# Sample attention of a two-layer encoder kernel: two groups of four heads on 64 partitions, or one group with two heads above each other on 128

## The reference

```
dots  = einsum('bqhd,bsd->bqhs', qi, ik_all)           # indexer: 8 heads x 64
score = einsum('bqhs,bqh->bqs', relu(dots), wi)
top_val, top_idx = top_k(where(admissible, score, -inf), k_top)
logits = einsum('bqngd,bqknd->bqngk', qg, k_sel) * HEAD_DIM ** -0.5   # 8 heads, 2 KV heads
p = softmax(where(valid, logits, -inf))
o = einsum('bqngk,bqknd->bqngd', p, v_sel)
```

## Time and profile before

| what | value |
|---|---|
| runs | 1450.54, 1449.7, 1452.48 us |
| profiled execution | 1449.31 us, its span 1447.5 us |
| busy TensorE / VectorE / ScalarE / GpSimd | 1253.6 / 569.4 / 368.4 / 152.4 us |
| chain that ended last | PE 69%, DVE 11%, DMA 7%, ACT 6%, issue 3% |
| mean granted TensorE clock | 0.914 of full speed |
| attention, layer 0 / layer 1 | about 314 to 416 us / about 1021 to 1121 us of the span |

### The profile page before, as it was taken

How to read it: one execution, slowest core, us unless ns; L and a number is a source line. 1 busy time by engine, 2 the same in 40 slices (tenths; PEclk the granted TensorE clock), 3 DMA queues, 4 the chain that set the end, 5 groups by cost and what they waited for, 6 DMA issues and landing times.

```text
span 1447.5 us, 16324 instructions
## 1 busy us (share of the span) xinstructions
PE 1253.6 (87%) x6291; PEld 733.4 (51%) x6291; DVE 569.4 (39%) x1478; ACT 368.4 (25%) x861; POOL 152.4 (11%) x218
## 2 busy tenths in 40 slices
PE   4898699987889998999837989899686999999990
PEld 0452254543545586777523533454345457777760
DVE  1227689123236531111107257980323455111115
ACT  2214120035741111111114133001468111111111
POOL 0312050010000150000020113200100011000002
PEclk7899899997999999999967989899858999999995
DMA  9428997260960479999953120224121016799985
GB/s 362 133 69 324 352 341 228 82 228 5 313 230 30 160 211 386 356 369 365 325 184 115 59 71 30 65 67 137 35 56 25 0 68 221 252 365 361 369 289 210
DMA packets 136887, 283.95 MB, mean 196 GB/s; under 512 B 11581, under 2 KB 91877, under 8 KB 130409
## 3 DMA queue, kind: packets, MB, share of 16 engines
q1 hardware_dynamic: 116128, 208.66, 42.7%
q0 software_dynamic: 8352, 42.50, 8.5%
q10 hardware_dynamic: 12329, 31.74, 6.2%
HBM read 236.86 MB, written 52.40 MB: 200 GB/s over the span
## 4 chain that ended last, share of the span: by engine, by line
PE 69%; DVE 11%; DMA 7%; ACT 6%; issue 3%; SPq 2%; ACTq 1%; POOLq 0%; POOL 0%; DVEq 0%
PE ps L508 44%; PE ps L813 9%; PE ps L518 5%; PE ps L671 3%; DMA W<-in_w_gate 3%; PE ps L732 3%; ACT arena L1194 2%; SPq L419 2%; DMA X<-in_x_sample 2%; DVE arena L1498 2%; PE ps L859 2%; DVE small L1497 1%; DVE arena L1537 1%; DVE arena L1588 1%; PE ps L632 1%
## 5 line engine op out<-in xcount | busy, mean ns | idle before, releaser
L508 PE MATMUL ps<-W,arena 128*128 128x256 f32 (+1 forms) x1280 | 348.1, 428 | 10.3 <-DMA W<-in_w_up 5.2
L508 PEld LDWEIGHTS ps<-W,arena 128*128 128x128 f32 x1280 | 242.2, 193 | 85.4 <-issue 49.9
L508 PE MATMUL ps<-W,hT 128*128 128x512 f32 (+3 forms) x480 | 195.0, 563 | 9.7 <-DVE gt L1369 6.6
L518 PE MATMUL ps<-C,arena 128*128 128x128 f32 (+3 forms) x835 | 118.4, 282 | 55.6 <-DVE arena L1417 18.1
L813 PE MATMUL ps<-W,hT 128*128 128x512 f32 (+1 forms) x320 | 144.7, 606 | 5.7 <-ACT hT L1251 5.7
L518 PEld LDWEIGHTS ps<-C,arena 128*128 128x128 f32 (+3 forms) x835 | 95.6, 148 | 96.6 <-issue 36.1
L508 PEld LDWEIGHTS ps<-W,hT 128*128 128x128 f32 (+1 forms) x480 | 87.4, 186 | 110.3 <-issue 83.4
L508 PE MATMUL ps<-hT,W 128*128 128x128 f32 (+1 forms) x512 | 129.4, 414 | 7.1 <-ACT arena L1118 7.1
L508 PEld LDWEIGHTS ps<-hT,W 128*128 128x128 f32 x512 | 79.1, 193 | 58.4 <-issue 50.5
L1805 DVE TENSOR_TENSOR arena<-arena,ps 128x256 f32<-128x256 f32 x32 | 13.5, 421 | 221.7 <-ACT arena L1292 221.7
L813 PEld LDWEIGHTS ps<-W,hT 128*128 128x128 f32 (+1 forms) x320 | 57.1, 183 | 79.9 <-issue 73.6
(11 more groups left out here) (250 smaller groups left out, 1174.1 us busy)
## 6 DMA issues: line engine op xcount, KB each, us to landing
W<-in_w_ada SPq DMA_DIRECT2D x48, 1024.0 KB, 7.4
W<-in_w_gate SPq DMA_DIRECT2D x32, 1024.0 KB, 10.6
W<-in_w_up SPq DMA_DIRECT2D x32, 1024.0 KB, 13.1
W<-in_w_down SPq DMA_DIRECT2D x32, 1024.0 KB, 7.8
y_d<-arena ACTq DMA_DIRECT2D x33, 512.0 KB, 7.3
W<-in_w_in SPq DMA_DIRECT2D x16, 1024.0 KB, 8.5
arena<-x_d SPq DMA_DIRECT2D x31, 512.0 KB, 11.5
arena<-arena SPq DMA_DIRECT2D x128, 79.2 KB, 2.1
```

Source lines behind the costliest of these rows:

```text
L508: ins = T.matmul(out, l, r, start=n == 0, stop=n == len(pairs) - 1, skip_group_check=True)
L518: count(T.transpose(o, i, ident[0:m, 0:m]), done if n == len(outs_ins) - 1 else None)
```

## The change

The sample's eight heads become one group, so `GROUPS` has nine members: 0 and 1 are tile 0, 2 is the sample, 3 and 4 are tile 3, 5 and 6 tile 2, 7 and 8 tile 1. A job of the sample's group is now two heads: the first head's 64 queries lie on partitions 0 to 63 of a bank, the second's on 64 to 127, each written by its own matmuls (same row half of the array, other column half). Masks, exponentials, scaling and turns of this group work on 128 partitions, the copies to `pT` are 512 wide, and each product with the values has 128 columns (two heads). The mask is copied once to partitions 64 to 127. The ada parts run at steps 1 to 8 (they were at 2 to 9). The square root is still at step 7 and the block of loads still at step 3.

```diff
-        GROUPS = [(t, g) for t in ATTN for g in range(2)]
+        GROUPS = [(t, g) for t in ATTN for g in range(2 if t < 4 else 1)]
...
-            return job % 3 if job < 8 else job % 2 if job < 16 else (job + 2) % 3
+            return job % 2 if GROUPS[job // 4][0] == 4 else job % 3
...
-                            pe.wait_ge(L["ttr"], job - 1 if 2 <= n <= 4 else job - 2)
-                        q = qT[hp, i, tokens(t)]
+                            pe.wait_ge(L["ttr"], job - 1 if 2 <= n <= 3 else job - 2)
                         if t == 4:
-                            T.matmul(ps[2 + job % 2][0:DEC, 0:DEC], q, kT[1][hp, 1024:1088], start=True, stop=True)
-                        T.matmul(ps[logit_bank(job)][0:rows_of(t), 0:b - a], q, kT[1][hp, a:b], start=True, stop=True).then_inc(L["lgt"], 1)
+                            for side in range(2):
+                                rows, q = slice(64 * side, 64 * side + DEC), qT[hp, 2 * (j // 2) + side, tokens(t)]
+                                T.matmul(ps[2 + job % 2][rows, 0:DEC], q, kT[1][hp, 1024:1088], start=True, stop=True, skip_group_check=True)
+                                ins = T.matmul(ps[logit_bank(job)][rows, 0:b - a], q, kT[1][hp, a:b], start=True, stop=True, skip_group_check=True)
...
-                    if l == 0 and 2 <= n < 6:
-                        pe.wait_ge(L["ttr"], 16)
-                        ada(ps[3], U_ADA4, range(2 * (n - 2), 2 * (n - 2) + 2), 3)
-                    if l == 0 and n >= 6:
+                    if l == 0 and 1 <= n < 5:
+                        pe.wait_ge(L["ttr"], 12)
+                        ada(ps[3], U_ADA4, range(2 * (n - 1), 2 * (n - 1) + 2), 3)
+                    if l == 0 and n >= 5:
...
-                            heads = pT[0:kn, c, 0:4 * m].rearrange("p (a g t) -> p a g t", a=2, g=2)
                             for a in range(2):
-                                ins = T.matmul(ps[6 + n % 2][64 * a:64 * a + 64, q * m:(q + 1) * m], v, heads[:, a, q, :],
+                                if t < 4:
+                                    heads = pT[0:kn, c, :].rearrange("p (a q t) -> p a q t", a=2, q=2)[:, a, q, :]
+                                else:
+                                    heads = pT[0:kn, c, :].rearrange("p (j q a t) -> p q a j t", j=2, q=2, a=2)[:, q, a]
+                                ins = T.matmul(ps[6 + n % 2][64 * a:64 * a + 64, q * P:(q + 1) * P], v, heads,
...
-                        S.copy(pT[0:kn, c, 0:4 * m], ps[4 + job % 2][0:kn, 0:4 * m]).then_inc(L["pta"], 1)
+                        S.copy(pT[0:kn, c, :], ps[4 + job % 2][0:kn, :]).then_inc(L["pta"], 1)
...
-                    if l == 0 and n == 7:
+                    if l == 0 and n == 6:
                         keep_mod(3)
...
                             chain(V.tensor_scalar(sc, sc, MARK, -BIG, ALU.not_equal, ALU.mult))
+                            if t == 4:
+                                chain(V.tensor_copy(msk[64:64 + DEC, MSK_AT[t]:MSK_AT[t] + n], sc))
```

More of the change, by code:

```diff
@@ L311, in u_tail @@
             return ps[7][:, at:at + P].rearrange("p (a c) -> p a c", a=2)
-        GROUPS = [(t, g) for t in ATTN for g in range(2)]
-        PT0 = [sum(len(chunks_of(t)) for t, _ in GROUPS[:n]) for n in range(11)]
+        GROUPS = [(t, g) for t in ATTN for g in range(2 if t < 4 else 1)]
+        PT0 = [sum(len(chunks_of(t)) for t, _ in GROUPS[:n]) for n in range(len(GROUPS) + 1)]
         def logit_bank(job):
-            return job % 3 if job < 8 else job % 2 if job < 16 else (job + 2) % 3
+            return job % 2 if GROUPS[job // 4][0] == 4 else job % 3
         def rope(eng, E, rows, r, t0, t1, heads, scratch, s_chain, n_chain, done, count):
@@ L727, in logits @@
                         if job >= 3:
-                            pe.wait_ge(L["ttr"], job - 1 if 2 <= n <= 4 else job - 2)
-                        q = qT[hp, i, tokens(t)]
+                            pe.wait_ge(L["ttr"], job - 1 if 2 <= n <= 3 else job - 2)
                         if t == 4:
-                            T.matmul(ps[2 + job % 2][0:DEC, 0:DEC], q, kT[1][hp, 1024:1088], start=True, stop=True)
-                        T.matmul(ps[logit_bank(job)][0:rows_of(t), 0:b - a], q, kT[1][hp, a:b], start=True, stop=True).then_inc(L["lgt"], 1)
+                            for side in range(2):
[3 more added lines that the diff above has]
+                        else:
+                            ins = T.matmul(ps[logit_bank(job)][:, 0:b - a], qT[hp, i, tokens(t)], kT[1][hp, a:b], start=True, stop=True)
+                        ins.then_inc(L["lgt"], 1)
                 tj = [0]
@@ L760, in _ @@
                         o = bank_for_turn()
-                        turn([(o[0:kn, i * m:(i + 1) * m], PR[0:m, 4 * (n % 2) + i, c * P:c * P + kn]) for i in range(4)], L["pt"])
+                        turn([(o[0:kn, i * P:(i + 1) * P], PR[:, 4 * (n % 2) + i, c * P:c * P + kn]) for i in range(4)], L["pt"])
                     if n + 2 < len(GROUPS):
                         logits(n + 2)
-                    if l == 0 and 2 <= n < 6:
-                        pe.wait_ge(L["ttr"], 16)
-                        ada(ps[3], U_ADA4, range(2 * (n - 2), 2 * (n - 2) + 2), 3)
-                    if l == 0 and n >= 6:
+                    if l == 0 and 1 <= n < 5:
+                        pe.wait_ge(L["ttr"], 12)
+                        ada(ps[3], U_ADA4, range(2 * (n - 1), 2 * (n - 1) + 2), 3)
+                    if l == 0 and n >= 5:
                         pe.wait_ge(s_adae, 5)
-                        ada(ps[3], U_ADA5, range(2 * (n - 6), 2 * (n - 6) + 2), 4)
+                        ada(ps[3], U_ADA5, range(2 * (n - 5), 2 * (n - 5) + 2), 4)
                     if n >= 2:
@@ L1203, in normalised @@
                         h = S_INV + 4 * (n % 2) + i
-                        r = PR[0:m, 4 * (n % 2) + i, 0:NKEYS[t]]
-                        ins = S.mul(r, r, small[0:m, h:h + 1])
+                        r = PR[:, 4 * (n % 2) + i, 0:NKEYS[t]]
+                        ins = S.mul(r, r, small[:, h:h + 1])
                     ins.then_inc(L["pn"], 1)
@@ L1210, in outputs @@
                     t, g = GROUPS[n]
-                    m = rows_of(t)
                     act.wait_ge(L["pv"], n + 1)
-                    S.copy(hT[:, g:g + 3:2, t * P:t * P + m],
-                           ps[6 + n % 2][:, 0:2 * m].rearrange("p (j t) -> p j t", j=2)).then_inc(L["on"], 1)
+                    o = ps[6 + n % 2][:, 0:2 * P]
+                    if t < 4:
+                        ins = S.copy(hT[:, g:g + 3:2, t * P:t * P + P], o.rearrange("p (j t) -> p j t", j=2))
+                    else:
+                        ins = S.copy(hT[:, 0:4, t * P:t * P + DEC], o.rearrange("p (j t) -> p j t", j=4))
+                    ins.then_inc(L["on"], 1)
                 exps(0)
@@ L1252, in _ @@
                                  scale=vT[:, 44 + c:45 + c]).then_inc(L["mixy"], 1)
-                outputs(9)
+                outputs(len(GROUPS) - 1)
                 if l == 0:
@@ L1577, in masked @@
                     t, g = GROUPS[n]
-                    m = rows_of(t)
-                    mk = C[0:m, K_M0:K_M0 + P] if t == 0 else msk[0:m, MSK_AT[t]:MSK_AT[t] + NKEYS[t]]
+                    m = P
+                    mk = C[:, K_M0:K_M0 + P] if t == 0 else msk[:, MSK_AT[t]:MSK_AT[t] + NKEYS[t]]
                     if n >= 2:
@@ L1590, in masked @@
                         if t == 4:
-                            ins = V.tensor_tensor_reduce(r[:, 512:576], ps[2 + job % 2][0:m, 0:DEC], mk[:, 512:576], 0.125, MARK,
+                            ins = V.tensor_tensor_reduce(r[:, 512:576], ps[2 + job % 2][:, 0:DEC], mk[:, 512:576], 0.125, MARK,
                                                          ALU.add, ALU.max, small[0:m, mx + 4:mx + 5])
@@ L1605, in inverses @@
                 def inverses(n):
[L1606 to L1608 removed]
+                    m = P
+                    s, q = S_SUM + 4 * (n % 4), S_INV + 4 * (n % 2)
                     dve.wait_ge(L["pexp"], n + 1)
@@ L1624, in _ @@
                         masked(n + 2)
-                    if l == 0 and n == 5:
+                    if l == 0 and n == 4:
                         add_bias(3, 3)
```

18 lines of the change are left out of this document (6 added, 12 removed).

## The result

The changed kernel takes 1432.22 us (median of four runs, 1425.78 to 1435.82) where the kernel before takes 1450.13 us beside it (four runs): a ratio of 0.9863 with a 95% interval of 0.9829 to 0.9897 (it is not the quotient of the two medians, which is 0.9876). The profiled execution took 1431.55 us, its span is 1429.7 us (17.8 us less than before).

A forecast was written before the change was run, and what follows sets the result against it. It took the attention's chain of waits round three engines, none full, as the bound, its speed hanging on TensorE's clock. 1449.31 - 7.9 - 8.9 + 3.6 + 2.2 + 0.5 = 1438.8, with 1.2 for the median 1440.0 us; range 1433 to 1448.

The forecast's parts named there:

- e2 later by: Start of group 2's (the sample's) exponentials, delayed by the second column half of each logits job: +0.6 us, bounds 0 and +2.0.
- e2 to e3: From the start of group 2's exponentials to group 3's (tile 3's first half): a period of 7.6 us.
- e3 to e4: From group 3's exponentials to group 4's (tile 3's second half), with group 2's five chunks: 13.6 us layer 0, 12.8 layer 1.
- e4 to e5: From group 4's exponentials to group 5's, with the sample's values: 9.0 us in layer 0, 9.4 in layer 1.
- step with the loads: Step 3, behind tile 2's first exponentials: the block of loads' stall comes back there, costing 2.5 us (layer 0), 2.1 (layer 1).
- the step behind it: The period after the step with the loads: same work as before, 7.5 us in layer 0 and 6.6 in layer 1.
- end of stage, longer by: Last exponentials to the Silu, with more work ahead of the square root: 3.6 us longer in layer 0, 2.2 in layer 1.
- the mask's copy: VectorE's copy of the mask, 0.45 us: costs 0.5 us in layer 1, 0 (or 0.5) in layer 0.
- Rival (a): The clock hardly drops in the attention, some 8 to 9 us less: 1431 to 1435 us; chance 0.12.
- rival (b): The sample's logits column halves run one after another, +1.4 us a layer: 1443 to 1444 us; chance 0.10.
- Rivals (c) to (e): Low clock past the sample's values, 1447, chance 0.10; no measurable change, 1449 to 1451, 0.06; slower, 1460, 0.04.
- (e): Slower: after the end of stage the output projection starts and stays at 1.2 GHz; 20 us more a layer gives 1460; chance 0.04.

The follow-up runs named there:

- its fillings: Kernel before plus three unread 128x512 matmuls in the wait of step 1's logits and three in step 2, both layers: 1444.6 us, ratio 0.9971.
- the combined kernel: Changed kernel with square root at step 6, seven transfers spread over steps 3 to 6, three unread matmuls in step 1's wait: 1417.43 us, ratio 0.9772.
- the first filling: Three unread 128x512 matmuls in step 1's wait, both layers; changed kernel with moved square root and spread loads: 1417.43 us with them, 1420.72 without.

## Why the prediction missed its range

**Direction and mechanism were right, one term was mis-sized.** The periods, in us, of the predicted steps and the profiled execution:

| term | layer 0: predicted, measured | layer 1: predicted, measured |
|---|---|---|
| e2 later by | 0.6, 0.1 | 0.6, 0.1 |
| e2 to e3 | 7.6, 7.78 | 7.6, 7.79 |
| e3 to e4 | 13.6, **9.73** | 12.8, **11.57** |
| e4 to e5 | 9.0, 9.42 | 9.4, 8.22 |
| step with the loads (old period plus 2.5, 2.1) | 11.2, 10.87 | 9.9, 10.97 |
| the step behind it (as before: 7.5, 6.6) | 7.5, 7.49 | 6.6, 7.35 |
| end of stage, longer by | 3.6, 3.82 | 2.2, 2.04 |

**The step that failed is "from e3 to e4".** For layer 0 I had TensorE at 1.2 GHz through the ada part, the values and the five chunks (8.7 us behind e3), and took "the middle, 4.9" for the logits behind them. The clock was back at 346 us, so this work hid under ScalarE's copies: the logits began to hold up e4 5.7 us behind e3 instead of 8.7, and from there to the exponentials it took 4.1 us, near the high clock's 3.97. That is 3.9 us, more than half of the 7.3 us by which the sum was too high (1438.8 against the profiled 1431.55). In the same paragraph stood "the clock may be back by then", for the reason that TensorE had no gap from 343 on; I carried that possibility into one half of the term and not into the other. In layer 1 the same term was 1.2 us too high, and e4 to e5, where the clock was back, 1.2 more; the two steps at the loads were 1.8 too low and take most of that back. Of the rest, 1.7 us are the terms for e2 and the mask's copy, of which the trace shows 0.2 for e2 and nothing that can be told of the mask, and 1.6 us lie outside the stretch from e2 to the projection, where I had forecast nothing and single executions differ by more. With the same kernel's second median, 1433.6 us, the number would have been inside the range; the term would have been as wrong.

**Rival (a) gave the right time, 1431 to 1435, for half of the right reason.** In part that is luck: its own terms (0.9 + 1.9, 1.6, 1.5 and 4) add up to 9.9 us and not to "8 to 9", and so to 1430. Its argument for (ada at step 1 fills a gap) is near what happened in layer 0, where TensorE had the ada part to do while the clock was low and it came back early; the run with ada a step later shows it. But the clock did drop, in both layers, and layer 1 stayed low for 13 us. Against (a) I had only that the gap before the drop is as long as before. That says when the clock falls and nothing of when it comes back. A chance of 0.12 was too low.

**What activity does to the clock.** With the waits of layer 1 filled the granted clock stays up and the step takes 9.73 us instead of 11.11; with ada a step later in layer 0 it stays at 0.50 until 352 us. This agrees with the Trainium skill, "TensorE: Matmul & The Clock Gate", Part 1: throttled by default, released by activity. The page spoke for (a), and I gave that no weight in the sum.

**The column halves.** The four matmuls of two jobs, each in its own quarter of the array, are eight records in 1.06 us, where two jobs of one matmul took 1.03. From the turn ahead of it e2 comes 0.1 us later than before (6.15 against 6.04 us). So rival (b) is out, and +0.6 was too much. (Rows 4 show the 1.03 us for a pair of jobs only; that a job alone takes as long, as the prediction says, is to be seen in layer 0's first sample group, where two jobs of 1.02 us start 0.75 us apart.) The second head of each job has its rows in common with the first, and its load added no time that can be seen here: all eight loads of the pair are over 0.23 us behind 331.58, while its matmuls run from 331.63 to 332.69. The Trainium skill, "TensorE: Matmul & The Clock Gate", Part 3 on packing small matmuls, lets a weight load overlap a running matmul only where the row group differs; here the measurement (1.06 us, where the rule would give about 2) decides against it.

**The end of the stage** came as worked out, as the moved square root shows. **The block of loads** came as worked out where the clock held behind it. In layer 1 it cost 1.1 us more than said, and 0.7 in the next step, because the clock fell, which one profile of the changed kernel has and the other not. In layer 0 both have it at 10.9 us, and three profiles of kernels that differ elsewhere at 12.4 to 12.6. I had priced a stall at its own length; a stall of TensorE may cost its length and half speed behind it.

**The mask's copy** cannot be told apart in these terms; no run tried it alone.

**Rivals (c) to (e)** did not happen. The projection began at 1.2 GHz as (e) says, but the clock rose soon: in layer 1 it is 0.50 from 1104 to 1106 us and 0.91 from 1106 to 1108.

## What to carry to other kernels

In a ring of engines with short matmuls, read the granted clock in each wait's wake before costing a step: the same step of layer 0 took 9.73 us here with one ada part ahead of it and 11.36 without, and a stall's price can be its length plus the half-speed work behind it. Where a clock term hangs on whether an engine has a gap, carry both clocks through the whole term and into the chances. When a loop loses an iteration, go through everything pinned to a step's number: the square root at `n == 7` gave back 6 us that one digit recovers, and the seven transfers in one step cost 4 to 5 by the steps of two traces.

## What I had not expected of the hardware

Useless work on TensorE can make the kernel faster. Two matmuls, 1.88 us together, in a wait of 2.85 us took 1.4 us off that step. The kernel before gained 4.2 us by its fillings (ratio 0.9971, 0.9953 to 0.999), and the medians of the combined kernel with and without the first filling are 3.3 us apart, on two chips.

The low clock comes and goes behind one and the same stall. In layer 0 of the kernel before the step with the loads takes 10.97 us in one profile and 13.22 or 13.33 in two others, one of them without any filling. So a filling is judged by its whole stretch, and by more than one profile.

The time between the two attentions, where no edit touches the code, varies from one execution to the next: from layer 0's Silu to layer 1's e2 the profiles show 631.50 us before, 630.66 after, 627.58 for the same kernel again, and 622.92 to 633.78 over all fourteen. Part of it is the wait for layer 0's expert weights. By the view of the costliest lines from 430 to 1010 us, the experts' matmuls were held up by the weights of the up projection for 2.3 us after, 2.0 in the repeated run, 8.1 where the loads are spread, and 1.4 in the combined kernel. This doesn't follow how early the experts start (the combined kernel reaches them before the one with the loads spread), and what sets it stays open. A difference of 3 us between single profiles isn't a finding here; the periods inside the attention mostly repeat to a few hundredths where the clock is the same, and differ by 1.3 to 2.3 us where it is not (the step with the loads).
